# A two-layer transformer kernel on one core: memory's value projection placed first, retention scores in pairs, layer two's norm factor behind its projections, cross scores inside the query projection

## The reference, cut to what matters

```python
xn = rms_norm(h, norm_mix_g)                      # x * rsqrt(mean(x*x) + eps) * g
sb_q, sb_k, sb_v, r_q, r_k, r_v, r_g = split(xn @ w_in)
y_sb  = stick_breaking_attention(...) @ w_sb_out   # 8 heads of 64
y_ret = retention(rotary(r_q), rotary(r_k), r_v)   # 8 heads: scores * decay, @ values
y_ret = y_ret * rsqrt(mean(y_ret**2) + eps) * ret_norm_g
y_ret = (silu(r_g) * y_ret) @ w_ret_out
h = h + (g_sb * y_sb + g_ret * y_ret) @ w_out      # sigmoid gates of xn
h = h + moe(rms_norm(h, norm_ffn_g))               # 16 experts, 2 per token
x = rms_norm(h, norm_final_g)
```

```python
h = rmsnorm(x, norm_mix_g_2); proj = h @ w_in_2    # keys/latent, q_idx, q_nope, q_rope, q/k/v_b
# index scores pick 128 keys per query; sparse attention over latents; dilated attention
x = x + heads @ w_out_2
hc = rmsnorm(x, norm_cross_g); m = rmsnorm(mem, norm_mem_g)
k, v = split(m @ w_kv_cross)                       # k_mem, v_mem
pc = softmax((hc @ w_q_cross) @ k.T / 16)          # 4 heads of 256, 256 keys
x = x + (pc @ v) @ w_o_cross
x = x + relu(rmsnorm(x, norm_mlp_g) @ w_up)**2 @ w_down
out = rmsnorm(x, norm_final_g_2)
```

## Time and profile before

| | us |
|---|---|
| median of 3 runs | 1790.32 (1783.61 to 1792.76) |
| the profiled execution's own time | 1788.25 |
| its span, first to last instruction | 1786.5 |
| TensorE busy | 1650.9 (92%) |
| VectorE / ScalarE / GpSimd busy | 900.5 / 746.2 / 662.6 |
| mean granted TensorE clock, share of full | 0.972 |
| DMA, mean over the span | 140 GB/s |

### The profile page before, as it was taken

The page is one execution under the profiler, slowest core; times in us unless marked ns, Lnnn a source line. Parts: engine busy times, 40 slices in busy tenths (PEclk is TensorE's granted clock), DMA queues, the critical chain, the costliest instruction groups (busy, mean ns, idle before and its releaser), DMA issues. The chain is left out here.

```text
span 1786.5 us, 21004 instructions
## 1 busy us (share of the span) xinstructions
PE 1650.9 (92%) x7928; PEld 1333.0 (75%) x7928; DVE 900.5 (50%) x1092; ACT 746.2 (42%) x886; POOL 662.6 (37%) x263
## 2 busy tenths in 40 slices
PE   4999999999999799999956989998998999999996
PEld 2888888578888788888845757756785788888885
DVE  4034210772464289998955568785423454141414
ACT  4244322343344487888733252376324332121211
POOL 2431264124443522333223534564440444444441
PEclk9999999999999899999978989999999999999998
DMA  4220142222226399999942222400230222322221
GB/s 158 106 72 24 59 142 96 81 71 94 94 99 262 144 421 405 391 384 387 389 178 72 87 83 81 151 8 1 102 112 23 94 71 97 115 94 95 94 94 47
DMA packets 46594, 249.23 MB, mean 140 GB/s; under 512 B 9440, under 2 KB 10208, under 8 KB 19904
## 3 DMA queue, kind: packets, MB, share of 16 engines
q1 hardware_dynamic: 40768, 237.85, 36.1%
q0 software_dynamic: 5184, 8.40, 1.3%
q10 hardware_dynamic: 576, 2.10, 0.3%
HBM read 238.15 MB, written 14.68 MB: 142 GB/s over the span
## 5 line engine op out<-in xcount | busy, mean ns | idle before, releaser
L148 POOL TENSOR_TENSOR w_lo<-raw,w_hi 128x2048 fp32r<-128x2048 f32 x101 | 464.8, 4602 | 740.9 <-ACT w_hi L142 740.8
L227 PE MATMUL psum<-x_hi,w_hi 128*128 128x512 f32 x872 | 346.5, 397 | 26.7 <-DVE x_lo L378 16.5
L228 PE MATMUL psum<-x_lo,w_hi 128*128 128x512 f32 x872 | 342.0, 392 | 0.0
L229 PE MATMUL psum<-x_hi,w_lo 128*128 128x512 f32 x872 | 341.9, 392 | 0.0
L142 ACT ACTIVATE w_hi<-raw 128x2048 fp32r<-128x2048 f32 x101 | 193.0, 1910 | 304.7 <-PE psum L229 304.2
L1555 DVE TENSOR_TENSOR moe_lo<-moe_w,moe_hi 128x2048 fp32r<-128x2048 f32 x99 | 225.6, 2291 | 54.0 <-ACT moe_hi L1496 53.0
L227 PEld LDWEIGHTS psum<-x_hi,w_hi 128*128 128x128 f32 x872 | 165.3, 190 | 71.5 <-DVE x_lo L378 15.4
L1496 ACT ACTIVATE moe_hi<-moe_w 128x2048 fp32r<-128x2048 f32 x99 | 189.6, 1916 | 24.0 <-PE psum L229 23.9
L229 PEld LDWEIGHTS psum<-x_hi,w_lo 128*128 128x128 f32 x872 | 165.3, 190 | 34.9
L228 PEld LDWEIGHTS psum<-x_lo,w_hi 128*128 128x128 f32 x872 | 165.8, 190 | 34.0 <-issue 0.7
L424 DVE TENSOR_TENSOR res<-res,psum 128x512 f32<-128x512 f32 x56 | 38.4, 687 | 217.6 <-PE psum L229 217.6
(11 more groups left out here) (339 smaller groups left out, 2872.1 us busy)
## 6 DMA issues: line engine op xcount, KB each, us to landing
raw<-in_w_dense SPq DMA_DIRECT2D x101, 1024.0 KB, 4.8
moe_w<-in_w_moe_ahead SPq DMA_DIRECT2D x54, 1024.0 KB, 10.7
moe_w<-in_w_moe SPq DMA_DIRECT2D x48, 1024.0 KB, 9.8
yrow<-expert_rows SPq DMA_DIRECT2D x8, 512.0 KB, 10.3
res<-in_x SPq DMA_DIRECT2D x4, 512.0 KB, 5.8
decay<-in_decay SPq DMA_DIRECT2D x8, 256.0 KB, 3.8
hn_rows<-hn_tok ACTq DMA_DIRECT2D x4, 512.0 KB, 8.6
out<-res SPq DMA_DIRECT2D x4, 512.0 KB, 2.7
```

The source lines that it names most:

```text
L148: pool.tensor_tensor(w_lo[c % RING][:, :], raw[c % RING][:, :], w_hi[c % RING][:, :].bitcast(F32), ALU.subtract).then_inc(lo_ready, 1)
L227: pe.matmul(out, lh, rh, start=first, stop=False)
L228: pe.matmul(out, lh, rl, start=False, stop=False)
L229: return pe.matmul(out, ll, rh, start=False, stop=last)
```

## The change

Nothing that is computed changes. Six places:

1. `v_mem` becomes the first layer. mem and chunk 0 are loaded ahead of x; mem times gain is split without its norm factor, chunk 0's rest is taken on VectorE, `norm1`'s matmul stands behind `v_mem`'s first chunk, and ScalarE's roundings of x are written out between `v_mem`'s copies. v goes to DRAM. Its factor per memory token (`mem_rstd_tok`) is applied when the probabilities are copied.
2. Retention scores are issued for two heads alternately; three buffers for the decayed scores; VectorE's norms of heads 1 to 3 follow the decays, those of heads 4 to 7 go between the gates of `ret_g`. `norm_mem`'s squares move behind `ret_g`.
3. Routing loses `v_mem`. The lists' hook is chunk 1 of `k_mem`; behind chunk 2 stand the transposes of the first experts' rows, with their roundings and subtractions; chunk 3's split goes ahead of the gathers.
4. The sum of the experts' rows joins the block of `project_*` (no barrier between). x times both gains is split there per block of 128 tokens. `r12` is multiplied into cos and sin tables, `c_kv`, `q_nope` (evacuated by VectorE), the index weights and `v_b`. cos32 and sin32 are loaded later.
5. Cross scores of heads 0 and 1 stand behind chunks 1 and 2 of `q_cross`, in banks 4 to 7; the later ones keep one head more in flight.
6. Two ring slots of the experts' rounded chunks change places in memory.

```diff
-LAYERS = [("sb_q", 2), ("sb_k", 2), ("sb_v", 2), ("ret_v", 4), ("ret_q", 2), ("ret_k", 2),
+LAYERS = [("v_mem", 4), ("sb_q", 2), ("sb_k", 2), ("sb_v", 2), ("ret_v", 4), ("ret_q", 2), ("ret_k", 2),
...
     def norm_qkv_sync(sp):
         sp.dma_start(cols[:, :], d["cols"]).then_inc(cols_landed, 16)
+        sp.dma_start(mem0[:, :, :], d["mem"]).then_inc(mv_landed, 16)
+        load_chunk(sp, 0)
         for g in range(4):
             sp.dma_start(res[:, 2 * g:2 * g + 2, :], d["x"][:, 2 * g:2 * g + 2, :]).then_inc(x_landed[g], 16)
-        load_chunk(sp, 0)
...
-        norm1.vector(dve, lambda e, kt: [e.wait_ge(x_landed[g], 16) for g in range(4)])
+        for kt in range(KT):
+            dve.wait_ge(mv_high, kt + 1)
+            dve.scalar_tensor_tensor(out=mv_lo[:, kt, :], in0=mem0[:, kt, :], scalar=col("mem", kt),
+                                     in1=mv_hi[:, kt, :].bitcast(F32), op0=ALU.mult, op1=ALU.subtract).then_inc(mv_low, 1)
+        split_lo(dve, 0)
+        norm1.vector_sum(dve, lambda e, kt: None)
+        for g in range(4):
+            dve.wait_ge(x_landed[g], 16)
+        norm1.vector_split(dve)
...
+        for kt in range(KT):
+            act.wait_ge(x_landed[kt // 2], 16)
+            norm1.square(act, kt)
         split_hi(act, 1, 0)
+        norm1.act_root(act)
+        v_mem_out(0)
+        v_mem_out(1)
+        split_hi(act, 2, 2)
+        v_mem_out(2)
+        norm_high(0)
+        norm_high(1)
+        v_mem_out(3)
+        split_hi(act, 3, 4)
+        norm_high(2)
+        norm_high(3)
+        v_mem_out(4)
+        norm_high(4)
+        norm_high(5)
+        v_mem_out(5)
+        split_hi(act, 4, 6)
+        norm_high(6)
+        v_mem_out(6)
+        norm_high(7)
+        v_mem_out(7)
+        split_hi(act, 5, 8)
...
-        norm1.pe(pe)
+        dense_pe(pe, "v_mem", mv_hi, mv_lo, token_major=True, norm=Parts(mv_low), hooks={0: lambda: norm1.pe(pe)})
         dense_pe(pe, "sb_q", x_hi, x_lo, norm=norm1)
...
-        def scores(h):
-            r = HD * (h % 2)
-            if h >= 2:
-                pe.wait_ge(rp_done, h - 1)
+        def scores(p):
+            if p >= 1:
+                pe.wait_ge(rp_done, 2 * p)
             for j in range(TB):
                 o, n = span(j)
-                mm = pe.matmul(Z[h % 2][:, o:o + n], ret_k[r:r + HD, h // 2, j * P:(j + 1) * P],
-                               ret_q[r:r + HD, h // 2, j * P:S], start=(j != 3), stop=True, skip_group_check=True)
+                for h in (2 * p, 2 * p + 1):
+                    r = HD * (h % 2)
+                    mm = pe.matmul(Z[h % 2][:, o:o + n], ret_k[r:r + HD, p, j * P:(j + 1) * P],
+                                   ret_q[r:r + HD, p, j * P:S], start=(j != 3), stop=True, skip_group_check=True)
...
+        for h in range(4):
             decayed(h)
+        decayed(4)
+        decayed(5)
+        retention_norm(dve, 0)
+        decayed(6)
+        decayed(7)
+        for h in range(1, HEADS - HEADS_NORMED_LATE):
+            retention_norm(dve, h)
...
         dense_pe(pe, "k_mem", m_high, m_low, n_tok=MEM, norm=norm_mem,
-                 hooks={0: lambda: [ranks_of_tokens(), rows(2), rows(3)], 2: lists_of_experts})
-        dense_pe(pe, "v_mem", m_high, m_low, token_major=True)
+                 hooks={0: lambda: [ranks_of_tokens(), rows(2), rows(3)], 1: lists_of_experts,
+                        2: lambda: [moe_rows_t(pe, 0, b) for b in range(2)]})
...
-        dense_pool(pool, "k_mem")
+        for b in range(RING):
+            split_lo(pool, FIRST_CHUNK["k_mem"] + 2 + b)
         first_rows()
-        for b in range(RING):
-            split_lo(pool, FIRST_CHUNK["v_mem"] + 2 + b)
...
+        def scaled(q):
+            dve.wait_ge(yt_added, 2 * q + 2)
+            if q >= 2:
+                dve.wait_ge(xq_low, q - 1)
+            dve.tensor_tensor(hy[q % 2][:, :, :], res[:, :, q * P:(q + 1) * P], wide(g12[:, :], [P, KT, P], 2), ALU.mult)\
+               .then_inc(y_scaled, 1)
+
+        def low(q):
+            dve.wait_ge(y_split, q + 1)
+            dve.tensor_tensor(x_lo[:, :, q * P:(q + 1) * P], hy[q % 2][:, :, :],
+                              x_hi[:, :, q * P:(q + 1) * P].bitcast(F32), ALU.subtract).then_inc(xq_low, 1)
...
             if q >= 1:
                 add(2 * q - 2)
                 add(2 * q - 1)
+                scaled(q - 1)
+            if q >= 2:
+                low(q - 2)
         add(6)
         add(7)
+        scaled(3)
+        low(2)
+        low(3)
...
         dense_pool(pool, "q_nope")
+        pool.wait_ge(narrow_in, 32)
+        for table in (cos32, sin32):
+            pool.tensor_tensor(table[:, :], table[:, :], r12[:, :], ALU.mult).then_inc(tables_done, 1)
...
+        dense_pe(pe, "q_cross", x_hi, x_lo, norm=norm_cross,
+                 hooks={0: lambda: norm_cross.pe(pe), 1: lambda: scores(0), 2: lambda: scores(1)})
+        pe.wait_ge(bank_free, FIRST_TILE["o_cross"] + 4)
         for h in range(CH_HEADS):
             transposes(h)
             if h + 2 < CH_HEADS:
```

624 lines of the change are left out of this document (338 added, 286 removed).

## The result

The changed kernel takes 1770.8 us (median of 4 runs, 1770.0 to 1771.4), the kernel before 1789.6 in the same session. The ratio is 0.990, with a 95% interval of 0.988 to 0.992: 1% faster. The forecast was 1768 with a range of 1756 to 1781.

What follows compares the result with a forecast made beforehand. TensorE's work plus its pauses was taken as the bound. Terms +22 - 27 - 5.5 - 1 - 6 + 1.5 - 5.5 = -21.5 took 1788.25 to 1766.8, stated as 1768 for the median; range 1756 to 1781.

Steps and rivals of the forecast that it cites:

- Start, +22: Start, up to `sb_q`: with the value projection first, `sb_q` starts at 53.8 against 31.4; +22 us, +16.5 at best.
- Routing, -27: Routing to the first expert matmul: `v_mem` leaves, a new gather pause of some 4 us comes; -27 us.
- Retention, -5.5: Retention: scores of two heads run together, 2.6 us instead of 4.6, less new pauses; 41.5 us for 47, -5.5.
- `ret_g` and `gate_ret`, -1: After retention: TensorE's 0.7 us wait for the memory norm goes, ScalarE's squares stand ahead of `gate_ret`'s first chunk; -1 together.
- Combine, -6: Layer two, sum of expert rows to `keys`: x split inside the sum, `keys` unpaced, next chunk ready earlier; -6 us.
- Project, +1.5: Layer two's projections: GpSimd's table scalings +2, one-column matmuls and small scalings +0.4, `q_nope` evacuation off ScalarE -0.9; +1.5 us.
- Cross, -5.5: Cross attention: scores 0 and 1 move inside `q_cross`, the first softmax pause goes, later waits shrink to two of 1.3; -5.5 us.
- A: Start and combine: GpSimd's subtractions delay VectorE little, 5.5 and 6 us less; 1756 us; chance 0.12.
- B: `ret_g`, start and combine: GpSimd's subtractions delay VectorE more, 14 to 18 us together; about 1783; chance 0.13.
- C: Retention: the two heads' score matmuls don't overlap; +8 us, 1776; chance 0.06.
- D: Routing: the gather lands in 8.7 us; +6.6 us, 1775; chance 0.06.
- E: Start and retention: new pauses lower TensorE's granted clock for long, some 40 us; 1808; chance 0.05.

Runs made afterwards that it cites:

- the one after it: On the kernel with the gain in the sums: expert rows loaded before both weight chunks, chunk 0's low part on VectorE, chunk 1 split behind the last block; 1764.4 us.
- the pairs: Changed kernel with retention's value blocks, then means of squares, taken two heads at a time, the next scores between the means; 1768.1 us.
- the hand-over by banks: Changed kernel with retention's means two heads at a time, plus four decay buffers and the first two heads' scores multiplied PSUM bank by bank; 1769.1 us.

## Why the prediction came out right, point by point

- **Bound and method.** TensorE's work plus its pauses, stage by stage, held: every gain and loss above is one of the two, once the granted clock is counted into the work. So did reading each term where its wait ends last.
- **Start, +22: right, +23.35**, with each step of the walk within 0.8 us. Part of that is luck: the walk counts 5.8 us of matmuls a chunk, but the chunk behind the pause of 4.61 took 7.6 (28.61 to 36.20), at a granted clock of 0.50 until about 32.5. And the size that was missed is the clock's too: `sb_q` itself took 45.4 us for 43.7 unpaced, with no pause inside it. Behind the pause of 3.81 its first eight matmuls start 0.43 us apart for 0.23, at a granted clock of 0.5 until about 56.5, which makes the 1.7 us. The last `x_lo`, held until 58.6, was not waited for. The range's end without holds, +16.5, is nearly what the kernel with VectorE's splits shows (+15.9: retention at 332.2 for 316.4), but there each split is shorter as well (2.3 for 4.6).
- **Routing, -27: -24.6.** The gather's pause is 5.12 and another of 1.49, for 4; the end of `k_mem` and the transposes came where the walk had them. What failed is the barrier, taken as 2.33 from the earlier trace rows: TensorE's pause there is 3.85, ended by nothing that the trace shows, and the experts took 1.0 more than before (286.2 for 285.2), all of it in their first 72 matmuls (19.4 for 18.4 us), whose first 8 us ran at a granted clock of 0.63 for 0.76. Why 3.85 stays open; it is 3.84 to 3.89 in every kernel of this study that has the change.
- **Retention, -5.5: -2.7.** Three terms. The pair was undersold (2.43 for 2.6). "1 for the first hand-over and the last mean" and "1 of new pauses" missed the four pauses of 0.98: with one head's scores between two value blocks, ScalarE's root had been hidden; in pairs half of these covers are gone. And the granted clock over retention fell from 1.00 to 0.96 (1.15 us in the second block and 0.5 in the values behind it), which I had only as a rival of 40 us.
- **`ret_g` and `gate_ret`, -1: +0.95.** The late norms cost TensorE nothing, as forecast: no pause in `ret_g`. But the squares of the memory norm on ScalarE delay a chunk: the pause of 1.38 at 451.27. I had named it and netted it too low: the pause of 0.66 in `ret_g` went, as forecast, 1.38 came, and four one-column matmuls.
- **Combine, -6: -8.7.** On the axis of before VectorE's last subtraction ends at 964.1, for the 965 of the walk: the hold was sized right. The miss is the step behind it: I had the last sums at 968, 3 us behind VectorE, and they end at 965.1, 1 us behind. The run with the gain in the sums and the one after it show what was still to be had in this stage: 13.3 us.
- **Project, +1.5: +1.3**, and near in its terms: GpSimd's two scalings (1.31 and 1.44 us) and its chunk hold VectorE's index sum 1.8 us longer, for 2 (two of its instructions take 1.30 for 0.48 each, the first 4.35 for 4.21); the one-column matmuls are eight, not four, and take 0.9 for 0.4; and the wait of TensorE ahead of that is 1.21 for 2.56, 1.35 less for 0.9.
- **Cross, -5.5: -5.7**, right in size and in its terms: the first pause is 0.79 for 2.86 (I had none), the two later ones 1.36 and 1.35 for the 1.3 forecast, and the slow value block went from 5.31 to 3.70. The run with the scores behind shows that the move of the scores is worth 2.5 of it; which of the other edits in that stage gave the rest is open.
- **`w_uk` to `out2`, not forecast, -2.0**, of which 1.7 in the attention. The code is the same and so are its pauses; TensorE's granted clock over the long middle of the stage is higher. The two stretches, before and after:

```profile
1165.00:1228.00 63.00, 62.05 (x336) 39.53 (x334) 55.79 (x133) 48.70 (x136) 38.21 (x40) 0.98 0.00 1
...
1154.50:1217.00 62.50, 60.55 (x333) 38.39 (x330) 56.94 (x135) 49.56 (x138) 39.37 (x41) 1.00 0.00 1
```

- **The rivals.** A and B, the hold catching little or more: neither, it was sized right at the start and in the combine. C, pairs that don't overlap: out, by 1.57 us a pair. D, a gather of 8.7 us: out, the pause is 5.1. E, the clock: its mechanism is real and small here, 1 to 2 us at the pauses of the start and retention, not 40.
- **The signs.** As named: first projection matmul at 13.62 for 14, `sb_q` at 53.1 for 54, a score pair 2.43 for 2.6, no pause in `keys`, none in `ret_g`. Missed: the first expert matmul at 620.6 for 613 (the misses of the start, of retention, of `gate_ret` and of routing added up), retention 44.3 us long for 42, and a pause of 0.79 ahead of the first cross transposes for none. One sign of failure did show, though not in the row named for it: that row has the same digits before and after, but over retention alone the granted clock is 0.96 for 1.00, and over `sb_q` alone as well.

## What to carry to other kernels

Before work is handed to VectorE, look at what GpSimd does at that time: an instruction with two inputs in SBUF, or a copy or one-input multiply from SBUF to SBUF, lasts until GpSimd's own instruction ends (4.47 us for 0.69 with two inputs, 4.21 for the copy), and taking the work away from GpSimd altogether can be faster even if VectorE then does all of it (11.5 us more of work, done 6.7 us earlier). When a block of work that stood between two dependent steps is moved or merged, ask for each step on the other engines what had hidden it, and which load or rounding stands behind the one that is now late: three fixes here (the pairs, the hand-over by banks, the combine) were first eaten, in part or whole, by the next wait in such a queue. A list of waits that names an engine whose instruction ended 0.02 us before the pause did is a hint, not a cause.

## What the runs showed of the hardware

- VectorE under GpSimd's SBUF subtraction (4.61 us): held to 0.15 to 0.56 us past its end are two-SBUF-input instructions (even of 128 columns, 4.07 us, and even into PSUM, 4.48) and copies and one-input multiplies from SBUF to SBUF (4.21); not held are reductions (0.69), a copy from SBUF to PSUM (0.70), a reciprocal (3.35) and a memset (0.48).
- Two matmul streams of 64 rows on the two halves of the array, issued in turn: 16 matmuls (2560 columns) in 2.43 us, for 4.00 when issued head by head.
- The price of a pause in granted clock is not fixed: the same 3.37 us ahead of the same block gave 1.00, 0.66 and 0.50 of full speed over it (2.43, 3.58 and 4.63 us) in three kernels whose TensorE code is the same up to there and that differ by a shift in time. An experiment of a few us must be read in its stage, not in its total.
